# A two-layer attention block with split fp32 weights: the remainders of the layers' weights, one in four by GpSimd before, all by VectorE

## The reference, cut to what matters

```
for l in range(2):
    h = rmsnorm(x, pre_norm_g[l])
    z = h @ w_in[l]                  # q_lat, kv_lat, k_pe, gb, gc, xin, q_mem, gate
    q = rmsnorm(q_lat) @ w_uq[l];  kv = rmsnorm(kv_lat) @ w_ukv[l]
    a_out = mla_attention(q, k, v)   # 8 heads
    c_out = short_gated_conv(gb, gc, xin, conv_w[l])
    m_out = memory_attention(q_mem, rmsnorm(mem), w_mk[l], w_mv[l])   # 4 heads
    y = concatenate([a_out, c_out, m_out]) * silu(gate)
    x = x + rmsnorm(y @ w_o[l], post_norm_g[l])
# second block: modulation vectors silu(c) @ w_mod (2048 x 12288) + b_mod
x = x + g1 * rmsnorm(fourier_mix(modulate(rms_norm(x))) @ w_fnet)
x = x + g2 * rmsnorm(square(relu(modulate(rms_norm(x)) @ w_mlp_in)) @ w_mlp_out)
```

## Time and profile before

| | |
|---|---|
| time, median of 3 runs | 1854.69 us (1853.36 to 1854.78) |
| span of the profiled execution | 1848.7 us |
| mean granted TensorE clock | 0.983 |
| PE busy | 1752.7 us (95%) |
| DVE busy | 1234.3 us (67%) |
| ACT busy | 844.2 us (46%) |
| POOL busy | 260.0 us (14%) |
| HBM traffic | 410 MB, 222 GB/s over the span |

### The profile page before, as it was taken

How to read it: one execution, slowest core, us unless ns; L and a number is a source line. 1 busy time by engine, 2 the same in 40 slices (tenths; PEclk the granted TensorE clock), 3 DMA queues, 4 the chain that set the end, 5 groups by cost and what they waited for, 6 DMA issues and landing times.

```text
span 1848.7 us, 30984 instructions
## 1 busy us (share of the span) xinstructions
PE 1752.7 (95%) x11521; PEld 1603.2 (87%) x11521; DVE 1234.3 (67%) x1343; ACT 844.2 (46%) x1149; POOL 260.0 (14%) x159
## 2 busy tenths in 40 slices
PE   3999999999999999999989989999999999999997
PEld 3998989987789999999768869987998799889985
DVE  6887787999788768789984555555455445545554
ACT  5546445533463554454335445443444344434442
POOL 5322111124242211121420001000000000000000
PEclk9999999999999999999999999999999999999998
DMA  6795878899659587789971544556455555555553
GB/s 223 228 343 179 290 239 270 285 320 320 237 180 333 190 300 236 258 282 334 328 253 69 201 141 160 183 183 204 160 183 199 188 178 185 186 185 183 183 202 114
DMA packets 211770, 411.98 MB, mean 223 GB/s; under 512 B 9088, under 2 KB 23712, under 8 KB 210848
## 3 DMA queue, kind: packets, MB, share of 16 engines
q1 hardware_dynamic: 210480, 407.51, 65.3%
q10 hardware_dynamic: 1136, 2.39, 0.4%
HBM read 407.75 MB, written 2.11 MB: 222 GB/s over the span
## 4 chain that ended last, share of the span: by engine, by line
PE 60%; issue 21%; DVE 10%; POOL 5%; DMA 3%; ACT 1%; DVEq 0%; POOLq 0%; ACTq 0%; SPq 0%
PE acc L319 56%; DVE modacc L932 5%; POOL wlo L312 3%; PE M L319 3%; DMA modw<-in_w_mod 2%; DVE wlo L312 1%; DVE X L829 1%; POOL memr L494 0%; DVE modacc L929 0%; DVE otok L785 0%; DMA pos<-in_positions 0%; PE M L1192 0%; POOL sc L481 0%; ACT whi L304 0%; POOL memr L487 0%
## 5 line engine op out<-in xcount | busy, mean ns | idle before, releaser
L304 ACT ACTIVATE whi<-raw 128x1024 fp32r<-128x1024 f32 (+2 forms) x576 | 592.9, 1034 | 787.6 <-PE acc L319 730.8
L312 DVE TENSOR_TENSOR wlo<-raw,whi 128x1024 fp32r<-128x1024 f32 (+2 forms) x504 | 640.5, 1276 | 457.9 <-ACT whi L304 439.0
L319 PE MATMUL acc<-Hhi,whi 128*128 128x256 f32 x2272 | 653.3, 288 | 12.4 <-DVE wlo L312 6.2
L319 PE MATMUL acc<-Hhi,wlo 128*128 128x256 f32 x2272 | 645.2, 284 | 0.0
L319 PE MATMUL acc<-Hlo,whi 128*128 128x256 f32 x2272 | 645.2, 284 | 0.0
L319 PEld LDWEIGHTS acc<-Hhi,whi 128*128 128x128 f32 x2272 | 438.1, 193 | 20.0 <-issue 11.9
L319 PEld LDWEIGHTS acc<-Hlo,whi 128*128 128x128 f32 x2272 | 438.3, 193 | 0.4
L319 PEld LDWEIGHTS acc<-Hhi,wlo 128*128 128x128 f32 x2272 | 438.2, 193 | 0.0
L932 DVE SCALAR_TENSOR_TENSOR modacc<-modw,cv,modacc 128x512 f32<-128x512 f32 x360 | 312.3, 868 | 18.0 <-DMA modw<-in_w_mod 7.4
L319 PE MATMUL acc<-whi,Yhi 128*128 128x512 f32 x768 | 303.6, 395 | 11.8 <-DVE wlo L312 11.8
L319 PE MATMUL acc<-wlo,Yhi 128*128 128x512 f32 x768 | 301.5, 393 | 0.0
(11 more groups left out here) (202 smaller groups left out, 1527.0 us busy)
## 6 DMA issues: line engine op xcount, KB each, us to landing
modw<-in_w_mod SPq DMA_DIRECT2D x192, 512.0 KB, 5.8
raw<-in_w_in SPq DMA_DIRECT2D x72, 1024.0 KB, 5.4
raw<-in_w_mlp_in SPq DMA_DIRECT2D x64, 1024.0 KB, 5.5
raw<-in_w_mlp_out SPq DMA_DIRECT2D x64, 1024.0 KB, 5.0
raw<-in_w_o SPq DMA_DIRECT2D x32, 1024.0 KB, 7.8
raw<-in_w_fnet SPq DMA_DIRECT2D x16, 1024.0 KB, 5.0
raw<-in_w_mk SPq DMA_DIRECT2D x8, 1024.0 KB, 5.2
raw<-in_w_mv SPq DMA_DIRECT2D x8, 1024.0 KB, 6.5
```

Of the source, the lines that this page charges most:

```text
L304: nc.scalar.activation(whi[s % HIR][:, 0:n], raw[u % RAW][:, (s % 2) * n:(s % 2) * n + n], ACT.Copy).then_inc(hi_ready, 1)
L312: unit.tensor_tensor(wlo[u % RAW][:, part], raw[u % RAW][:, part], whi[s % HIR][:, 0:n].bitcast(F32), ALU.subtract).then_inc(done, 1)
L319: return nc.tensor.matmul(o, a, b, start=start, stop=stop, skip_group_check=True)
```

## The change

`POOL` loses its share of the remainders. `DVE` makes the remainder of every half of the layers, in the same place of its program (first thing in step s, for half s + 3). `PE` waits for one counter (`lo_ready`) in place of two. One wait is added: before `ACT` writes `rows`, it waits until `POOL` has made all of its normed memory tokens, since both lie in the same memory.

```diff
-LO_POOL = 4
...
-        lo_pool = sem("lo_pool")
...
-        LO0 = DEPTH * (LH - LH // LO_POOL)
+        LO0 = DEPTH * LH
...
-        def of_pool(s):
-            return s % LO_POOL == LO_POOL - 1
...
                     if s == 0:
                         pool.wait_ge(o_ss, l + 1)
                         rstd(OS, OM, OR, l * 4 + 2, o_rstd)
-                    if of_pool(s + AHEAD):
-                        split_lo(pool, nc.gpsimd, l * LH, s + AHEAD, half_of(s + AHEAD), lo_pool)
                     if s == 0:
                         norm_mem(2, 1)
...
             act.wait_ge(r_T, 1)
+            act.wait_ge(mem_xn, DEPTH * KT + 8)
             nc.scalar.activation(rows[:, :], M[0][0:2 * KT, 0:P], ACT.Copy).then_inc(rows_ready, 1)
...
                 for s in range(LH + 1):
-                    if s < LH and not of_pool(s + AHEAD):
+                    if s < LH:
                         split_lo(dve, nc.vector, base, s + AHEAD, half_of((s + AHEAD) % LH), lo_ready)
...
                 def wait_lo(s):
 
-                    if of_pool(s):
-                        pe.wait_ge(lo_pool, l * (LH // LO_POOL) + s // LO_POOL + 1)
-                    else:
-                        pe.wait_ge(lo_ready, l * (LH - LH // LO_POOL) + s + 1 - (s + 1) // LO_POOL)
+                    pe.wait_ge(lo_ready, l * LH + s + 1)
```

## The result

| | before | after |
|---|---|---|
| time, median | 1854.74 us (4 runs) | 1826.80 us (4 runs, 1825.39 to 1829.43) |
| ratio, 95% interval | | 0.9847 (0.9833 to 0.9862) |
| span of the profiled execution | 1848.7 us | 1824.0 us |
| DVE busy | 1234.3 us | 1218.3 us |
| POOL busy | 260.0 us | 88.0 us |

The kernel is 27.9 us faster by the medians, and 24.8 us by the two spans (1848.74 and 1823.96 before rounding). The time was forecast at 1833.5, with 1824 to 1848 as the range.

What follows compares the result with a forecast made beforehand. PE was taken to bound the kernel, waiting for DVE in places. Gains of 12.7 + 5.9 + 2.6 = 21.2 us off the 1848.7 us span gave 1827.5, plus 6.0 to the median 1833.5 us; range 1824 to 1848.

Steps and rivals of the forecast that it cites:

- What bounds: Two layers: PE busy 1752.7 of 1848.7 us; only its waits count, and DVE is near its limit at the wo halves.
- What POOL's remainders cost DVE: Each POOL remainder in the wo halves holds one DVE instruction 1.9 to 2.2 us; excess over both groups 73 us.
- the step that decided the sign: DVE beside POOL's remainders: the change slows the kernel if a hold is worth less than 1.14 us.
- The wo halves: Ahead of half 140: holds removed less remainders added, 8.1 + 7.0 us; 12.7 after the loads, bounds 0 and 20.
- 2.4 us for the loads: Wo halves: loads must keep up with a faster PE, so 1.2 us was taken off each layer's gain.
- The gc halves: Holds behind PE's waits at 135 to 146 go: 4.0 us in layer 0, 1.9 in layer 1, bounds 1.9 and 8.
- The lower clock behind that wait: Gc halves of layer 1: PE's lower clock may add up to 2.3 us, left out of the sum.
- The start of a layer: Residual and half 4 come earlier: 1.4 us in layer 0, 1.2 in layer 1, sum 2.6, bounds 0 and 4.6.
- From the span to the median: Whole kernel: 6.0 us between span and median, added to the forecast span of 1827.5 to give 1833.5 us.
- The loads as the bound: Rival, wo halves: loads or the order of SP take the gain there, perhaps 5 us left, about 1841 us; chance 0.20.
- No change: Rival: PE's waits are set by something right behind DVE, such as ACT's rounding; 1852 to 1856 us, chance 0.08.
- Slower: Rival: long DVE instructions come from, say, the full DMA; nineteen added remainders cost 22 us, 1876 us, chance 0.10.

Runs made afterwards that it cites:

- the repeated run: The changed kernel, with nothing altered, run again beside the last experiment on the same chip: 1825.14 us, ratio 0.9834 to the kernel before.

## Why the prediction was right, point by point

**What bounds.** That DVE's 67% is a full engine at the wo halves, and that only PE's waits count, held. Work added to DVE there (fourteen subtractions, 13.9 us) and holds put back there (25.2 us) both cost time. DVE was busy for 113 of the 122 us from 364 to 486 us before the change. POOL's instructions, which nobody waited for, counted only through DVE.

**What POOL's remainders cost DVE.** Nine holds of 1.9 to 2.2 us were read off. Fourteen of them put back cost 25.2 us, 1.8 each after the slack, and the excess of both groups went. DVE's busy time was forecast at 1215 to 1240 and is 1218, but the sum written beside it, 80 us added and 70 taken away, would have made it grow. The 72 new remainders are 84 us by their means, and the total fell by 16, so 100 us went: 72 in the two groups of the earlier trace rows, the rest in groups that I hadn't counted, such as `meml` (28.0 to 21.1 us) and the single-input `modacc` (15.9 to 11.5). The hold was the step that decided the sign, and it is shown: a hold is worth more than the 1.14 us that a remainder costs, measured at 1.0 to 1.2.

**The wo halves.** The net of holds and remainders was forecast at 8.1 + 7.0 = 15.1 us ahead of half 140. From the start of half 112 to that of half 143 the gain is 6.8 + 7.3 = 14.1 us, and 7.5 + 7.1 in the repeated run. From the 15.1 I took 2.4 us for the loads. This term was mis-sized: with the loads of `w_mod` halved, the wo halves gain 1.0 us in layer 0 and 0.2 in layer 1. I read it so, without a run that shows it, that the queue had more room than its 368 GB/s suggested because the stretch ahead (213 GB/s before, 351 after) filled first.

**The gc halves.** 5.9 forecast, 5.9 measured: that the sums agree is luck in part. The split is 3.4 and 2.5 instead of 4.0 and 1.9. Half 36 still waits 0.56 us in layer 0, and in layer 1 the wait for `sqlat` shrank from 1.92 to 1.04. The lower clock behind that wait, which I had left to the range, is in the measured 2.5: it was granted 0.50 over 4.1 us before and 0.60 after. In six profiled executions that do the changed kernel's work in these halves (this one, the repeated one and four of the experiments) layer 0 gained 2.0 to 3.6 us there and layer 1 1.6 to 4.8.

**The start of a layer.** Layer 0 gained 1.2 of 1.4, but by another way than I had written: DVE's new remainder of half 3 now holds POOL's root back. POOL before, and then the timeline after, POOL and DVE:

```profile
32.78 0.20 POOL L479 TENSOR_TENSOR sc<-sc 128x2 f32<-128x2 f32 x1 [2.19 <-DVE sc L846]
...
32.82 1.16 POOL L474 TENSOR_TENSOR sc<-sc 128x2 f32<-128x2 f32 x1 [2.19 <-DVE sc L840]
...
32.70 1.23 DVE L310 TENSOR_TENSOR wlo<-raw,whi 128x1024 fp32r<-128x1024 f32 x1
34.88 5.47 DVE L823 SCALAR_TENSOR_TENSOR X<-otok,sc,X 128x2048 f32<-128x2048 f32 x2 [0.95 <-POOL sc L476]
```

An addition of two columns takes 1.16 us beside DVE's remainder and took 0.20 us before, with DVE idle. The residual starts 1.0 us later than in the earlier trace rows and takes 5.47 instead of 7.13, so it ends 0.7 us earlier and not 1.4. The other 0.5 us come from the remainder of half 4, which takes 1.21 us in place of 1.74. I had said that the remainder of half 3 falls into a wait, as if it cost nothing. The wait at 44 was to shrink to about 1.4 us; it is 2.44, since PE comes to it 0.8 us earlier.

Layer 1 gained 2.9 instead of 1.2, of which 1.4 is the lower clock: behind the wait of 3.79 us the granted clock was 0.64 over 4.4 us, and behind the shorter one of 2.29 it is 1.00. In the repeated run of the changed kernel the wait is 3.44 us and the clock behind it 0.61 again, so those 1.4 us belong to single executions.

**From the span to the median.** I put 6.0 us around the span. It is 1.8: the changed kernel's profiled run of 1825.74 us has a span of 1823.96. By that the profiled execution of before took about 1850.5 us, below its median; later runs of the same kernel went from 1850.6 to 1861.3 us. The forecast of 1833.5 us was 6.7 too high. Of this, 3.6 is the sum (21.2 for 24.8 by the spans) and 4.2 the 6.0 in place of 1.8; the changed kernel's profiled run lies 1.1 below its own median, which takes as much back.

**The rivals.** The loads as the bound: no, the time is 1826.8 and not 1841, and half of the modulation loads is worth 5.7 us by the medians, of which the trace places 1.2 in the wo halves. No change: no. Slower, because the long instructions come from the DMA: no; they are gone in the changed kernel with the queue at a share of 0.97 to 1.03, and POOL's readers bring them back. The added wait of ACT and the single counter weren't tried by themselves; with both in place, POOL's fourteen subtractions brought back nearly the whole time of the kernel before.

## What to carry to other kernels

Work given to GpSimd to relieve VectorE isn't free for it: where both read SBUF, one GpSimd instruction can stop a VectorE instruction for most of its own length, here 1.9 us for a relief of 1.14. Compare the mean of a group with its undisturbed instructions, and look at what GpSimd did beside the long ones. An engine that is 67% busy over the whole can be nearly full for 120 us on end (here 113 of 122). Slack inside a chain, as in the uq halves here, can't be filled with work from elsewhere.

## What the runs showed of the hardware

- Beside a POOL subtraction of 128x1024 in SBUF, a DVE subtraction of that size took 3.11 to 3.43 us for 1.22, a pair of 128x512 multiply-adds 3.55 to 3.69 for 1.53, and a 128x512 multiply with one tensor input 2.62 for 0.48. Beside a POOL memset of 128x1022 (0.95 us) the DVE subtraction took 1.22.
- The hold works the other way too: a POOL addition of 128x2 took 1.16 us beside a DVE remainder and 0.20 us in the kernel before, with DVE idle.
- The queue moved 368 GB/s over 34 us on this one core, with the matmuls running, and 371 over 3.6 us in the changed kernel.
